# Where twelve short modulation steps are slipped in: five of them moved from the stick-breaking heads to the top-k search, with four PSUM banks for filling work there

## The reference, cut to what matters

```python
rel = jax.nn.relu(jnp.einsum('bqhd,bsd->bqhs', qi_blk, ki))
score = jnp.einsum('bqhs,bqh->bqs', rel, wi_blk) * idx_scale
_, sel = lax.top_k(score, k_sel)
```

## Time and profile before

| | |
|---|---|
| time of three runs | 3676.97 us median (3672.37 to 3677.84) |
| the profiled execution, its own time | 3678.62 us |
| its span, first to last instruction | 3677.3 us |
| PE busy | 3397.8 us (92%) |
| PEld busy | 2662.3 us (72%) |
| DVE busy | 1725.6 us (47%) |
| ACT busy | 1286.2 us (35%) |
| POOL busy | 924.0 us (25%) |
| granted TensorE clock, mean | 0.961 of full speed |

### The profile page before, as it was taken

The page is one execution under the profiler, slowest core; times in us unless marked ns, Lnnn a source line. Parts: engine busy times, 40 slices in busy tenths (PEclk is TensorE's granted clock), DMA queues, the critical chain, the costliest instruction groups (busy, mean ns, idle before and its releaser), DMA issues.

```text
span 3677.3 us, 44516 instructions
## 1 busy us (share of the span) xinstructions
PE 3397.8 (92%) x17216; PEld 2662.3 (72%) x17216; DVE 1725.6 (47%) x3184; ACT 1286.2 (35%) x2202; POOL 924.0 (25%) x397
## 2 busy tenths in 40 slices
PE   6998998999999898899989779999999998889999
PEld 4765776777767677677778457888888656667887
DVE  3348224434335622543489774322264665543234
ACT  3333323333333331433342442322243445543232
POOL 2222121124312212112333002322364100024443
PEclk9999998999999998999999888999999999999999
DMA  3442012123453211213312001121242110012322
GB/s 140 177 147 76 29 64 78 55 88 112 144 185 117 71 40 63 69 56 111 102 52 86 12 1 46 64 69 58 66 153 86 48 51 1 1 52 92 102 93 80
DMA packets 87907, 288.48 MB, mean 78 GB/s; under 512 B 10000, under 2 KB 20624, under 8 KB 86800
## 3 DMA queue, kind: packets, MB, share of 16 engines
q1 hardware_dynamic: 86688, 275.80, 22.0%
q10 hardware_dynamic: 1008, 9.83, 0.7%
HBM read 281.40 MB, written 4.19 MB: 78 GB/s over the span
## 4 chain that ended last, share of the span: by engine, by line
PE 54%; DVE 6%; ACT 2%; issue 2%; POOL 0%; DVEq 0%; ACTq 0%; POOLq 0%
PE psum L307 13%; PE psum L308 13%; PE psum L309 13%; PE psum L306 11%; PE psum L3253 1%; DVE mla_cols L3342 1%; PE psum L3241 1%; PE psum L1110 0%; DVE h_low L562 0%; DVE mixed_features L2479 0%; PE psum L3219 0%; DVE ml_weights L2787 0%; DVE rounded L550 0%; ACT mla_probs L3298 0%; ACT k_feat L3289 0%
## 5 line engine op out<-in xcount | busy, mean ns | idle before, releaser
L402 POOL TENSOR_TENSOR weights_low<-weights_loaded,weights_high 128x1024 fp32r<-128x1024 f32 (+2 forms) x380 | 910.3, 2396 | 2736.5 <-ACT weights_high L384 2703.9
L307 PE MATMUL psum<-h_high,weights_high 128*128 128x512 f32 (+1 forms) x2400 | 920.5, 384 | 48.5 <-DVE h_low L562 26.5
L308 PE MATMUL psum<-h_low,weights_high 128*128 128x512 f32 (+1 forms) x2400 | 891.3, 371 | 0.0
L309 PE MATMUL psum<-h_high,weights_low 128*128 128x512 f32 (+1 forms) x2400 | 890.2, 371 | 0.0
L307 PEld LDWEIGHTS psum<-h_high,weights_high 128*128 128x128 f32 x2400 | 460.4, 192 | 147.7 <-issue 50.3
L384 ACT CAST weights_high<-weights_loaded 128x1024 fp32r<-128x1024 f32 (+2 forms) x380 | 392.4, 1033 | 479.9 <-PE psum L309 402.5
L308 PEld LDWEIGHTS psum<-h_low,weights_high 128*128 128x128 f32 x2400 | 460.3, 192 | 83.0 <-issue 10.0
L309 PEld LDWEIGHTS psum<-h_high,weights_low 128*128 128x128 f32 x2400 | 458.9, 191 | 78.8
L3609 DVE TENSOR_TENSOR act_low<-ffn_act,act_high 128x512 fp32r<-128x512 f32 (+1 forms) x66 | 143.1, 2168 | 137.7 <-ACT act_high L3579 137.6
L307 PE MATMUL psum<-act_high,weights_high 128*128 128x512 f32 (+1 forms) x528 | 187.7, 356 | 8.4 <-DVE act_low L3609 6.2
L309 PE MATMUL psum<-act_high,weights_low 128*128 128x512 f32 (+1 forms) x528 | 187.5, 355 | 0.0
(11 more groups left out here) (441 smaller groups left out, 5111.4 us busy)
## 6 DMA issues: line engine op xcount, KB each, us to landing
weights_loaded<-stream_dram SPq DMA_DIRECT2D x472, 512.0 KB, 3.3
weights_loaded<-stream_dram SPq DMA_DIRECT2D x80, 128.0 KB, 3.2
weights_loaded<-stream_dram SPq DMA_DIRECT2D x24, 384.0 KB, 3.0
weights_loaded<-stream_dram SPq DMA_DIRECT2D x8, 272.0 KB, 5.7
x<-x_dram SPq DMA_DIRECT2D x1, 2048.0 KB, 9.0
arena_mem<-mem_dram ACTq DMA_DIRECT2D x2, 1024.0 KB, 6.5
x<-x_dram ACTq DMA_DIRECT2D x1, 2048.0 KB, 7.8
x_kept_dram<-x ACTq DMA_DIRECT2D x1, 2048.0 KB, 11.0
```

Source lines behind the costliest of these rows:

```text
L307: pe.matmul(out, a.high, b.high, start=start, stop=False)
L308: pe.matmul(out, a.high, b.low, start=False, stop=False)
L309: return pe.matmul(out, a.low, b.high, start=False, stop=stop)
L402: pool.tensor_tensor(self.low[s][:, 0:size], raw[:, 0:size], self.high[s][:, 0:size], ALU.subtract).then_inc(*g.event("weights_low").up(po ...
```

## The change: what it does

Four fills less per layer in the stick-breaking heads (the one ahead of `weights`), and 18 places instead of 15 in the search: one more in each of the three query blocks, for PE after the four score matmuls, for DVE after the mask, and for ACT between the Relu of head 1 and that of head 2. So modulation items 8 to 12 of a layer are left when `dsa` begins (before, only item 12). `queue_among` puts them between the others: item 8 ahead of the first gate, 9 to 12 each after one gate and its product. Item 8 falls to the fill among the `dsa` projections (where item 12 was), items 9 to 12 to the search. During the search the index scores take banks 0 to 3 in turn (before, the six of the branch) and the filling work banks 4 to 7.

```diff
+def queue_among(g, eng, l, b):
+
+    later = g.later[g.who[id(eng)]]
+    ada, later.items = later.items, []
+    queue_merge(g, eng, l, b)
+    for k, item in enumerate(ada):
+        later.items.insert(3 * k, item)
...
     rope_tensor(g, key("k", 1), turn, g.c.perm64)
+    narrow, index, g.spare = g.spare, Turn(0, 4), Turn(4, 4)
     for i in range(1, QT):
         m_keys = (i + 1) * P
         for hd in range(IDX_HEADS):
-            b = g.claim(key("index", i, hd), turn.next(1))
+            b = g.claim(key("index", i, hd), index.next(1))
...
+        fill_tensor(g)
         for r in range(TOPK // 8):
             if r % 3 == 2:
                 fill_tensor(g)
+    g.spare = narrow
...
                 *S("drained").up(act, key("index", i, hd)))
+            if hd == 1:
+                fill_scalar(g)
...
             *S("indexed").up(dve))
+        fill_vector(g)
         for r in range(TOPK // 8):
...
             scores(hd + 1)
-        fill_tensor(g)
         weights(hd)
         fill_tensor(g)
         weigh(hd)
...
             logs(hd + 1)
-        fill_scalar(g)
         weights(hd)
         fill_scalar(g)
...
-        fill_vector(g, 2)
+        fill_vector(g)
         gated(hd)
...
     if b == 1:
         queue_mem(g, eng, l, b)
+    elif b == 2:
+        queue_among(g, eng, l, b)
+        queue_fox(g, eng, l)
     else:
         queue_merge(g, eng, l, b)
-        if b == 2:
-            queue_fox(g, eng, l)
```

## The result

The changed kernel takes 3682.49 us (median of 20 runs, 3677.56 to 3686.87); the kernel before, run beside it, 3678.5 us (20 runs, 3671.61 to 3683.2). The ratio is 1.0013, with a 95% interval of 1.0007 to 1.0019. I forecast 3697.

What follows compares the result with a forecast made beforehand. PE was taken to bound the heads and softmax, DVE the search. Per layer -14.4 (heads) +4.6 (projections) +19.6 (search) +0 (softmax) = +9.8, over two layers +19.6 on 3677.0, so 3697 us; range 3676 to 3714.

Steps and rivals of the forecast that it cites:

- The softmax: Softmax behind the search: product 7 now exposed, fox items cover waits at the end; 0 us a layer, bounds -4 and +4.
- signs of being wrong: Gate 1 within 1 us of item 9's end, no DVE wait in block 2, or softmax moving over 4 us a layer.
- The heads: Stick-breaking heads: four fills removed from PE gain 14.4 us a layer, bounds 10.9 to 15.
- The projections: Projections of dsa: item 8 replaces the columns and delays the second query projection; 4.6 us a layer lost, bounds 1.85 and 6.
- The search, block 1: DVE waits 6.4 us for the Relu behind gate 0's Tanh, then 3.2 us for product 1; block 2 reached 8.5 late.
- Block 2: Search, block 2: the Relu waits for gate 2 behind the same chain; rounds start 17.7 us late, 1 us more for product 3.
- Block 3: Search, block 3: gate 4 ends before DVE asks for the Relu, so no new wait; search 19.6 us a layer later.
- The load: Gate chunks in the search: 7.4 us from issue to matmul by the trace row, preferred to the skill's 3.2 us landing estimate.
- Rival A: Search: same chains but mild, full clock after idle times, 6.9 us issue to matmul; 3679 to 3683 us; chance 0.12.
- Rival B: Search: weight ring keeps ahead, gates start as modulation items end, only block 1's 6.4 us stay; 3664 us; chance 0.09.
- Rival C: Search: PE stood on banks 6 and 7, four banks let it run ahead; -10 us a layer, 3657 us; chance 0.03.
- Rival D: Chains take 8 to 9 us under modulation loads, search +24, fox items meet ACT badly (+4); 3715 us; chance 0.16.

Runs made afterwards that it cites:

- experiment 1: b_shift in the table: kernel before with 14 instead of 15 filling places in the search, the last of query block 3 removed; 3664.64 us, ratio 0.996.
- experiment 2: b_pause in the table: kernel before with an item that does nothing put between product 7 and fox item 0; 3659.31 us, ratio 0.9949.
- experiment 3: a_late in the table: changed kernel with ACT's early fill of each query block moved behind the Relu of head 3; 3683.31 us, ratio 1.0009.
- experiment 4: a_banks in the table: changed kernel with the earlier bank rotation, six for the branch, 6 and 7 for filling; 3675.82 us, ratio 0.9992.
- late2v: late2 with DVE taking the last modulation item behind the last round and keep mask, not ahead of round 13; 3645.66 us, ratio 0.9914.
- experiment 5: a_first in the table: changed kernel with modulation items 8 to 12 all ahead of the first gate; 3674.14 us, ratio 0.9992.
- late2: Kernel before with fills of heads 0 and 3 dropped, none among projections, remaining modulation items behind product 6 in query block 3; 3648.71 us, ratio 0.9927.
- late3: As late2, but with three head fills dropped (heads 0, 1 and 3) and eight places in query block 3; 3659.14 us, ratio 0.9949.
- late4: As late2, but with all four head fills dropped and nine places in query block 3; 3664.44 us, ratio 0.9969.
- behind2: As late2, but modulation items behind gate 7, one more place in query block 3, first softmax place empty; 3657.11 us, ratio 0.9959.
- behind3: As behind2, but with three head fills dropped (heads 0, 2 and 3) and nine places in query block 3; 3664.07 us, ratio 0.9971.
- behind4: As behind2, but with all four head fills dropped; 3671.65 us, ratio 0.9985.

## Why the prediction was wrong, step by step

- **The softmax** is the step that failed: "the fox items reach one place further and cover waits at the end. I take 0, bounds -4 and +4." It measured -7.8 and -8.1 us in the two layers of the change itself (-5.2 and -5.4 up to the end of the softmax, the rest in the next branch's first gate), -7.85 a layer in experiment 1 and -9.6 in experiment 2, with the rest of the kernel untouched. The direction stands in the prediction's own sentence, and a move by more than 4 us was one of its signs of being wrong. What was missing is the price behind the wait: the earlier trace rows give that stage a clock of 0.88, and I had priced the clock in the search (7.85 us for a gate) but not here. 77 x 0.12 = 9.2 us of lower clock lay there to be recovered, though not how much of it would be. The two layers' 15.9 us are more than the 14.4 us between the forecast of +19.6 and the profiled +5.2.
- **The heads**: -14.75 measured in layer 0 (-16.3 in layer 1), -14.4 forecast. `weights` waits 0.37 us for DVE (forecast 0.6); from head to head PE needs 14.6 us (14.7). Right.
- **The projections**: +4.66 in layer 0 (+6.3 in layer 1), forecast +4.6. PE waits 2.64 us for L402 at 227.59 in the second query projection (2.7). Right.
- **The search, block 1**: from the first index sum to the first round it is 7.2 us longer than before (forecast 6.4). Issue to matmul 6.8 us (7.4), gate 8.0 (7.85), wait for product 1 2.8 (3.2). **Block 2**: against the first index sum the rounds are 17.95 us late (17.7). **Block 3**: no new wait. Search +19.44, forecast +19.6. Size and chain right. But the wording "it is the surest term" of the Relu's wait was wrong as a cause: experiment 3 takes it away and gains nothing measurable. It lies beside the gate chain; the sum was right because it followed the chain.
- **The load**: the chain from issue to matmul measured 6.8 us where my row gave 7.4, for the load landed within 265.65 - 262.40 = 3.25 us. The rule of the Trainium skill ("DMA: Bandwidth & Descriptors", anatomy of one DMA) gave 3.2 as an estimate, and this load agrees with it better than with the row that I took. But the section gives its figures for a DMA that GpSimd issues, which the prediction left out; these loads are issued by SP.
- **Rival A** has the nearest time (3679 to 3683), but not its mechanism: the clock did fall and the chains were not mild. **Rival B** is out (gates 1 to 3 start 3.5 to 4.7 us late). **Rival C** is out, with the sign reversed: in experiment 4 two banks are faster than four. The advice of the Trainium skill that stands there ("Perfetto Trace Analysis", Matmuls: rotate independent groups through banks) did not pay here: by experiment 4 the change is 0.2% slower with four banks for filling than with two. **Rival D** is out: the search is 19.4 us longer, not 24. (Its terms add up to +19.5 a layer, not +19, so to 3716 us.)
- **The rest**: behind that, each layer's later stages give some 1.6 us back, to -0.6 us at the end of the first block (at 1840 us). In this profile the changed kernel is then level with before; the +5.8 us that make the profiled +5.2 arise in the second block, whose code is the same (below). That it came out slower, as forecast, is by this profile not the work of the terms that I had summed; where the 4.0 us between the medians arise, one profile of each can't tell.

So 18.5 us lost up to the softmax in two layers (forecast 19.6), 15.9 given back in the softmax and the gate behind it, 3.2 behind that, and 5.8 lost in unchanged code: 5.2.

## What to carry to other kernels

A filling item's worth lies in which wait it covers, and where the clock falls behind a wait, as it did here, two waits of 2.4 us together were worth 5.4 us more up to the end of the softmax; look at the granted clock of every stage that the edit shifts items in, also far behind it. When two waits lead to the same point, price the path and not the waits: the removal of one (experiment 3) may be worth nothing. And an item moved to where an engine idles pays the price of its loads there; move as many as the loads allow (two here, not four). And before a gain is put down to an edit, follow it to the next wait: late2v's 2.3 us in the search came back as a longer wait for the next logits.

## What the runs showed of the hardware that was not expected

- **Unchanged code moves by up to 6 us.** The second block's instructions are the same in all these kernels. Start of the DVE instruction that begins at 1840 us before, and the end of the span, each as variant minus before:

| | at 1840 us | at the end | in between |
|---|---|---|---|
| changed kernel | -0.6 | +5.2 | +5.8 |
| b_shift | -15.6 | -13.3 | +2.3 |
| b_pause | -19.7 | -20.6 | -0.9 |
| a_late | -0.7 | +1.7 | +2.4 |
| a_banks | -6.9 | -0.9 | +6.0 |
| a_first | -7.6 | -5.1 | +2.4 |
| late2 | -29.1 | -23.1 | +6.0 |
| late3 | -24.5 | -18.5 | +6.0 |
| late4 | -15.3 | -15.9 | -0.6 |
| behind2 | -24.1 | -21.5 | +2.6 |
| behind3 | -16.0 | -16.9 | -0.9 |
| behind4 | -9.6 | -7.0 | +2.6 |
| late2v | -33.2 | -30.5 | +2.7 |

  It comes in steps, in the changed kernel +1.1 us near 2000 us, +2.7 between 2000 and 2400 us and +2.0 between 2800 and 3200. These are single executions, and the 20 runs of the kernel before differ by 11.6 us among themselves, so it may belong to the execution and not to the kernel; that was not tested. It bounds what a change in the first block can be read to from one profile, about 0.15%.
- **Waits of the same length cost differently.** 3.6 us of idle PE ahead of a modulation item left the gate behind at a clock of 0.95 (experiment 4, 5.8 us); 4.2 us directly ahead of the gate brought it to 0.68 (8.0 us). But 3.55 us directly ahead of gate 2 left it at 1.00 in a_late, and 3.52 us brought it to 0.67 in the changed kernel. Neither length nor place alone tells whether the clock falls; what does is not shown.
- **The modulation items' matmuls don't fix their pace.** Back to back they need 5.3 to 6.8 us each for 2 MB of weights (experiment 5), 2.7 in the heads. In experiment 5 the clock was at 0.50 and PE also waited for ACT's copy of the row (0.8 us); what the loads alone take was not separated.
